# Encoder trunk on one core: the right operands of the output projection's Strassen products made during the retention instead of during the output projection

## The reference

```python
D_MODEL, SEQ, DEPTH = 1024, 1024, 2
RET_HEADS, RET_HEAD_DIM, RET_CHUNK = 4, 128, 128

for layer in range(DEPTH):
    h = rms_norm(x, norm_g[layer])
    z = h @ w_in[layer]
    qa, ka, va, ga, qr, kr, vr, gr, gm = split_columns(z)
    ...                                         # branch A: attention, SiLU gate
    ya = (jax.nn.silu(ga) * oa) @ w_branch_attn[layer]
    ...                                         # branch B: rotary on qr, kr, then
    orr = bidirectional_retention(qr, kr, vr, lg_f, lg_b)
    orr = head_group_norm(orr, ret_gn_w[layer]).astype(dt)
    yb = (jax.nn.silu(gr) * orr) @ w_branch_ret[layer]
    gates = jax.nn.sigmoid(gm).reshape(b, s, 2, d)
    merged = gates[:, :, 0] * ya + gates[:, :, 1] * yb
    x = x + merged @ w_out[layer]
return rms_norm(x, final_norm_g)
```

## Time and profile before

| | |
|---|---|
| median of 3 runs | 1848.42 us (1846.0 to 1848.89) |
| the profiled execution, its own time | 1849.25 us |
| its span | 1847.4 us, mean granted clock 0.989 |
| busy: PE, DVE, ACT, POOL | 95%, 68%, 43%, 36% of the span |
| weight loads (PEld) | 84% |
| chain that ended last | PE 73%, DVE 16%, ACT 4%, issue 4%, DMA 2%, POOL 1% |
| DMA | 113 MB, mean 61 GB/s |

### The profile page before, as it was taken

The page is one execution under the profiler, slowest core; times in us unless marked ns, Lnnn a source line. Parts: engine busy times, 40 slices in busy tenths (PEclk is TensorE's granted clock), DMA queues, the critical chain, the costliest instruction groups (busy, mean ns, idle before and its releaser), DMA issues.

```text
span 1847.4 us, 30201 instructions
## 1 busy us (share of the span) xinstructions
PE 1755.8 (95%) x10592; PEld 1556.1 (84%) x10592; DVE 1264.8 (68%) x2626; ACT 801.0 (43%) x1791; POOL 672.2 (36%) x581
## 2 busy tenths in 40 slices
PE   6999999999999999998989999999999999999986
PEld 5887878899999888887787888889999998888875
DVE  6789678725543387769986876795345544867798
ACT  4478448722123243334344873683222223433333
POOL 0157227624233323223601771484224322232240
PEclk9999999999999999999999999999999999999998
DMA  7000000011011323224130001001011023222322
GB/s 270 24 12 13 28 23 24 25 46 47 23 34 35 131 70 96 81 93 157 46 118 24 24 1 50 12 13 47 24 46 45 27 88 114 71 78 86 131 80 92
DMA packets 136665, 113.08 MB, mean 61 GB/s; under 512 B 16480, under 2 KB 115040, under 8 KB 136544
## 3 DMA queue, kind: packets, MB, share of 16 engines
q1 hardware_dynamic: 134144, 106.20, 18.0%
q10 hardware_dynamic: 2400, 5.31, 0.8%
HBM read 90.52 MB, written 20.97 MB: 60 GB/s over the span
## 4 chain that ended last, share of the span: by engine, by line
PE 73%; DVE 16%; ACT 4%; issue 4%; DMA 2%; POOL 1%; SPq 0%; DVEq 0%; ACTq 0%; POOLq 0%
PE ps L758 17%; PE ps L760 17%; PE ps L759 17%; PE ps L894 5%; PE ps L883 4%; PE ps L907 3%; PE ps L909 3%; DVE xh L2173 2%; PE ps L1000 2%; DVE pT_lo L1804 2%; PE ps L984 1%; DVE nmx L1796 1%; DVE lsum L2151 1%; DVE us L1905 1%; ACT pp L1289 1%
## 5 line engine op out<-in xcount | busy, mean ns | idle before, releaser
L758 PE MATMUL ps<-w_hi,hT_hi 128*128 128x256 f32 (+1 forms) x1280 | 391.1, 306 | 13.0 <-DVE hT_lo L1669 4.4
L760 PE MATMUL ps<-w_hi,hT_lo 128*128 128x256 f32 (+1 forms) x1280 | 376.5, 294 | 0.0
L759 PE MATMUL ps<-w_lo,hT_hi 128*128 128x256 f32 (+1 forms) x1280 | 376.3, 294 | 0.0
L758 PEld LDWEIGHTS ps<-w_hi,hT_hi 128*128 128x128 f32 x1280 | 244.9, 191 | 17.9 <-DVE hT_lo L1669 6.1
L759 PEld LDWEIGHTS ps<-w_lo,hT_hi 128*128 128x128 f32 x1280 | 245.3, 192 | 0.3
L760 PEld LDWEIGHTS ps<-w_hi,hT_lo 128*128 128x128 f32 x1280 | 244.6, 191 | 0.0
L612 POOL TENSOR_SCALAR pp<-pp,rrc 128x1024 f32<-128x1024 f32 x128 | 144.0, 1125 | 161.0 <-DVE rrc L1809 155.1
L1804 DVE TENSOR_TENSOR pT_lo<-ps,pT_hi 128x512 fp32r<-128x512 f32 x256 | 164.2, 682 | 24.4 <-ACT pT_hi L1300 22.9
L558 POOL TENSOR_SCALAR w_hi<-raw 128x1024 fp32r<-128x1024 f32 x65 | 69.1, 1063 | 286.2 <-PE ps L760 250.0
L894 PE MATMUL ps<-idf,pp 128*128 128x128 f32 x1024 | 141.5, 278 | 18.4 <-DVE pT_lo L1804 12.3
L1796 DVE TENSOR_REDUCE nmx<-ps 128x1 f32<-128x1024 f32 x128 | 154.4, 1206 | 2.6 <-PE ps L883 2.6
(11 more groups left out here) (215 smaller groups left out, 4106.8 us busy)
## 6 DMA issues: line engine op xcount, KB each, us to landing
raw<-w_in SPq DMA_DIRECT2D x167, 256.0 KB, 3.2
xs<-xh SPq DMA_DIRECT2D x2, 4096.0 KB, 16.2
ys<-y_st SPq DMA_DIRECT2D x32, 256.0 KB, 2.1
hb<-ys SPq DMA_DIRECT2D x16, 512.0 KB, 4.4
xh<-xs SPq DMA_DIRECT2D x8, 1024.0 KB, 7.4
raw<-w_a SPq DMA_DIRECT2D x16, 256.0 KB, 3.2
raw<-w_r SPq DMA_DIRECT2D x16, 256.0 KB, 3.3
w<-w_o SPq DMA_DIRECT2D x4, 1024.0 KB, 6.1
```

Source lines behind the costliest of these rows:

```text
L758: nc.tensor.matmul(outp, ah, bh, start=(start and i == 0), stop=False)
L759: nc.tensor.matmul(outp, ah, bl, start=False, stop=False)
L760: last = nc.tensor.matmul(outp, al, bh, start=False, stop=(stop and i == len(pairs) - 1))
```

## The change

The right operands of a layer's seven products are now made while its retention runs, in 28 steps: four quarters of 128 rows in each quadrant (`k`, `K_R` = 4), and in each quarter the seven products in the order `R_ORDER`. A step makes 128x512 numbers of `hi` and of `lo`. It takes three engines: GpSimd's `right_sum` adds or subtracts two blocks (20 of the 28 steps; the others use a block as it is), ScalarE casts, VectorE subtracts (`right_lo`). One tile later ScalarE issues a DMA that stores `hi` and `lo` (512 KB) to a DRAM tensor `wos`. A quarter's raw weights (1 MB) come by a DMA on ScalarE's queue, `right_load(k)`: the first ahead of head 0's first pass, the others once the quarter before is used up.

The places are numbered 2·8·h + t in a first pass and + 8 in a second; there are 56 (the second pass of the last head has none). The table puts steps at k·13 + 2 + {0, 2, 3, 5, 6, 8, 9}: 2, 4, 5, 7 in the first pass of head 0, 17, 18, 20, 21, 23 in that of head 1, 33, 34, 36, 37 in head 2, 49, 50 in head 3, the other thirteen in second passes. The sum stands one place ahead, behind that tile's add and fill; the cast stands at the top of the tile on ScalarE, the subtraction at the top of the tile on VectorE.

In the output stage the whole of `right_sum`, `right_hi` and `right_lo` is gone. SyncE's `right_in(p)` loads the finished operand of a product, 2 MB in four DMAs, into a slot when it is free; TensorE waits for these DMAs (`o_r`) where it waited for `o_blo`. So 14 MB are stored and 14 MB loaded in each layer beside the 4 MB of `w_o` that were loaded before too. The retention's loops over heads on ScalarE, VectorE and GpSimd are written out instead of looped, TensorE's is unchanged.

```diff
+K_R = 4
+R_ORDER = (1, 5, 0, 2, 3, 4, 6)
+R_PLACES, R_LOAD = (0, 2, 3, 5, 6, 8, 9), 10
+R_AT = {2 + (R_LOAD + 3) * k + o: k * N_P + i for k in range(K_R) for i, o in enumerate(R_PLACES)}
+R_LOADS = {2 + (R_LOAD + 3) * k + R_LOAD: k + 1 for k in range(K_R - 1)}
...
 # GpSimd
+                def right_sum(place):
+                    if place + 1 not in R_AT:
+                        return
+                    n = R_AT[place + 1]
+                    blocks = RIGHT[R_ORDER[n % N_P]]
+                    if len(blocks) == 1:
+                        return
+                    pool.wait_ge(r_in, 16 * (L * K_R + n // N_P + 1))
+                    r_free(pool, L, n)
...
+                    nc.gpsimd.tensor_tensor(r_total(n), a, b, ALU.add if q > 0 else ALU.subtract).then_inc(r_sum, 1)
...
                                 fill_lo(i % 2, i, n0 + U_C + fills * N_C + N_C + i)
+                        right_sum(2 * T * h + t)
...
 # ScalarE
+                def right_steps(place):
+                    if place - 1 in R_AT:
+                        n = R_AT[place - 1]
+                        act.wait_ge(r_hi, L * N_R + n + 1)
+                        act.wait_ge(r_lo, L * N_R + n + 1)
+                        a, k = 2 * (n % 2), n // N_P
+                        act.dma_start(wos[R_ORDER[n % N_P], :, :, 512 * k:512 * k + 512],
+                                      quad(ur_lo, 4)[:, a:a + 2].bitcast(F32)).then_inc(r_out[n % 2], 16)
+                    if place in R_LOADS:
+                        right_load(R_LOADS[place])
+                    if place in R_AT:
...
+                        nc.scalar.copy(r_rows(n)[0], r_src(n)).then_inc(r_hi, 1)
...
                 def first_pass(h, done):
                     for t in range(T):
+                        right_steps(2 * T * h + t)
...
 # VectorE
+                def right_lo(place):
+                    if place in R_AT:
+                        n = R_AT[place]
+                        dve.wait_ge(r_hi, L * N_R + n + 1)
+                        hi, lo = r_rows(n)
+                        V.tensor_tensor(lo, r_src(n), hi.bitcast(F32), ALU.subtract).then_inc(r_lo, 1)
...
                 def first_pass(h, done):
                     for t in range(T):
+                        right_lo(2 * T * h + t)
                         if done is not None and 2 <= t <= 3:
                             cross(done, 2 * t - 4)
...
                 add_up(0)
-                right_lo(2)
                 left_lo(3)
                 add_up(1)
-                right_lo(3)
                 left_lo(4)
...
 # SyncE
+                for p in range(3, N_P):
+                    if p != 4:
+                        sp.wait_ge(o_done, L * (4 * N_P) + 4 * N_P + 4 * ({3: 0, 5: 1, 6: 2}[p] + 1))
+                    right_in(p)
```

More of the change, by code:

```diff
@@ L111, in build @@
 def build(nc, x, gains, w_in, qn, kn, decays, gn_w, w_a, w_r, w_o,
-          ident, rope_a, rope_r, dist, idx, xs, ys, out):
+          ident, rope_a, rope_r, dist, idx, xs, ys, wos, out):
     with ExitStack() as ctx:
@@ L168, in build @@
             pT_lo = sb(p2, "pT_lo", [2, T, 256], F32R)
+        with ExitStack() as pz:
+            sb(pz, "below_wo", [2 * SEQ])
+            wo_raw = sb(pz, "wo_raw", [4, 512])
         ur_hi = sb(ctx, "ur_hi", [KA, SEQ], F32R)
@@ L200, in build @@
             pp = sb(pp_, "pp", [3, SEQ])
-        with ExitStack() as pw:
-            w21 = sb(pw, "w21", [4, 512])
         hb = sb(ctx, "hb", [2, DM])
@@ L205, in build @@
             w12 = sb(pg, "w12", [4, 512])
+        with ExitStack() as pg:
+            first_r = sb(pg, "first_r", [4, 512], F32R)
         gB = sb(ctx, "gB", [DM])
@@ L249, in build @@
             "g_sum", "g_hi", "g_wd", "g_wp", "g_p", "g_a", "g_d", "g_t"))
[L250 to L253 removed]
+        o_r = [[sem("o_r%d%d" % (i, h)) for h in range(2)] for i in range(4)]
+        r_in, r_sum, r_hi, r_lo = map(sem, ("r_in", "r_sum", "r_hi", "r_lo"))
+        r_out = [sem("r_out0"), sem("r_out1")]
+        o_sum, o_ahi, o_alo, o_done, o_post = map(sem, ("o_sum", "o_ahi", "o_alo", "o_done", "o_post"))
         f_y = sem("f_y")
@@ L354, in build, with right_wide @@
         quad = lambda t_, a: t_[:].rearrange("p a (b c) -> p (a b) c", c=512)[:, a:a + 4]
-        w22 = raw[:].rearrange("p a k (b c) -> p (a k b) c", c=P).rearrange("p (a b) c -> p a (b c)", b=4)
-        w11, w11b = w1x[:, 0:4], w1x[:, 4:8]
-        right_raw = (w12[:], w11, w11b, w11b, w11, w22, w11)
+        def right_wide(p, h):
+            return 256 if p in IN_W and (p, h) != (0, 0) else 512
         def right_slot(p, h):
+            if (p, h) == (0, 0):
+                return first_r[:, 0:2], first_r[:, 2:4]
             if p in IN_W:
@@ L508, in _, with right_in @@
                 y_back(1)
-                def block(kh, c, k0=0, kn=4):
-                    src = w_o[bass.ds(L * DM, DM), c * 512:(c + 1) * 512].rearrange("(k p) c -> p k c", p=P)
-                    return src[:, 4 * kh + k0:4 * kh + k0 + kn]
+                def right_in(p, halves=(0, 1)):
+                    for h in halves:
+                        c = right_wide(p, h)
+                        for s, to in enumerate(right_slot(p, h)):
+                            src = wos[p, :, s, 1024 * h:1024 * h + 1024].rearrange("p (b c) -> p b c", c=c)
+                            sp.dma_start(to.bitcast(F32), src).then_inc(o_r[R_SLOT[p]][h], 16)
                 def x_block(r, c):
@@ L675, in _ @@
                 rotate(0, None)
-                with pool.Fori(0, RH - 1) as h:
+                for h in range(RH - 1):
                     fill_qk(h)
+                    for t in range(T):
+                        right_sum(2 * T * h + T + t)
                     rotate(h + 1, h)
@@ L1142, in last_product @@
                     pe.wait_ge(o_alo, L * (2 * N_P) + 2 * ORDER_A.index(p) + 2)
-                    pe.wait_ge(o_blo, L * (2 * N_P) + 2 * N_P + 2 * p + 2)
+                    for h in range(2):
+                        pe.wait_ge(o_r[R_SLOT[p]][h], 32 * (L * R_USES[R_SLOT[p]] + R_NTH[p] + 1))
                     for i in range(4):
@@ L1399, in second_pass @@
                             update(h, t - 1)
+                right_load(0)
                 first_pass(0, None)
-                with act.Fori(0, RH - 1) as h:
+                for h in range(RH - 1):
                     second_pass(h)
@@ L1941, in normed @@
                     V.tensor_tensor(oc[:, o], oc[:, o], g2[:, o], ALU.mult).then_inc(c_yg, 1)
+                def right_lo(place):
+                    if place in R_AT:
+                        n = R_AT[place]
+                        dve.wait_ge(r_hi, L * N_R + n + 1)
+                        hi, lo = r_rows(n)
+                        V.tensor_tensor(lo, r_src(n), hi.bitcast(F32), ALU.subtract).then_inc(r_lo, 1)
                 def keep_out(h, half):
+                    if h >= 2:
+                        for b in range(2):
+                            dve.wait_ge(r_out[b], 16 * (L + 1) * (N_R // 2))
                     dve.wait_ge(consts_in, NCONST)
@@ L1984, in _ @@
                 first_pass(0, None)
-                with dve.Fori(0, RH - 1) as h:
+                for h in range(RH - 1):
                     second_pass(h)
@@ L2189, in _ @@
                 merge_a(K - 1, 0)
-                right_lo(0)
                 give(K - 1, 4)
```

155 lines of the change are left out of this document (58 added, 97 removed).

## The result

The changed kernel takes 1894.92 us (median of 5 runs, 1894.18 to 1899.34), the kernel before 1848.89 in the same comparison: ratio 1.0252, interval 1.024 to 1.0263. It is slower by 46 us. The prediction said 1885, range 1862 to 1903, slower.

The account below looks back on a forecast made before the run. TensorE was taken to bound the retention, VectorE the output projection. From the profiled 1849.25, +57 for the retention, −24.2 for the output stages and +4 for the clock gave 1886.1, 0.8 over the median, so 1885; range 1862 to 1903.

Parts of the forecast that it names:

- What bounds what: Retention: TensorE full, 29.39 of 30 us; output projection: VectorE full, 10.00 of 10, TensorE with holes.
- Output stage: Output projections of both layers: TensorE's holes go, about 12.1 us a layer, −24.2 in all.
- What VectorE would shed: Output projection: VectorE loses fourteen subtractions and the slowdown beside GpSimd's sum, at least 18.6 of 90 us.
- Rivals 2 and 4: Output stage: 2, operands late, +3.5 a layer, 1892, chance 0.10; 4, half the gain, +12, 1897, 0.10 with Rival 3.
- Waiting in the retention: First passes: TensorE waits for the serial chain of each step, 28.5 us a layer, +57 in all.
- The hole at the third cross term: Head 1, first pass: TensorE's next cross waits for the banks of the first, 3.4 us.
- tiles 6 and 7: Head 1, first pass: rotations of tiles 4 and 5 come late for TensorE, 1.4 and 1.3, together 2.7 us.
- Second passes: Retention: the thirteen steps there cost nothing; if that cover fails, some 0.5 a step, 6 a layer.
- Clock: Granted clock falls after retention holes, 6.8 us; falls of the output stages go, about 3.4; taken as +4.
- Rival 3: Retention: the clock falls after every hole, +10 more, 1895; chance 0.10 together with rival 4 of the output stage.
- The page's exclusion: Retention: each of 20 sums could hold up a subtraction or scan step 1.3 us, 1 or 2 us more a head.
- Rival 1: Retention: TensorE's spare bank covers the chain, so it costs 0; 1824, chance 0.08.

Follow-up runs that it names:

- subtraction last: Changed kernel with VectorE's subtraction in first passes moved from the top of the tile to its end; 1845.75 us.
- transfers-alone kernel: Changed kernel without sums, casts, subtractions and the waits for them; loads and stores stay, a fixed copy is stored; 1821.69 us.
- the best order tried: Changed kernel with the subtraction at the end of the tile in first passes and the 28 steps at other places; 1835.96 us.

## Why the prediction was right, and where its sizes were off

**What bounds what.** Right. The output projection was VectorE's and its holes went; the retention was TensorE's, and its spare bank didn't cover the chain. That the same instructions in another order (subtraction last) give 1845.75 shows it for the retention, the transfers-alone kernel (1821.69) for the output projection.

**Output stage, forecast −24.2.** Measured −25.0. The two parts on which it rested are seen: no `o_r` wait in the products (no idle time over 0.05 us between 875.31 and 953.37, though most pieces of an operand, 512 KB each, landed 9.5 to 11 us after issue, with others issued around them), and VectorE 63.27 of 78.06 us, no longer full. What VectorE would shed was taken too small: 23.4 us went (86.68 less 63.27) where 18.6 of 90 were worked out; it bounded nothing any more either way. Rivals 2 and 4 fall.

**Waiting in the retention, forecast 28.5 a layer.** Measured 25.2 and 25.4 (27.5 and 27.9 less the 2.3 and 2.6 that stood there before). By head, layer 0, idle forecast and measured: 6.5 and 5.7, 8.7 and 7.9, 8.5 and 7.4, 4.8 and 4.1, each somewhat too large. In head 0 the step at place 4 was given a sum that it doesn't have (it uses a block as it is), and the first cast began at 377.1, which with this trace's 2.4 us of lead is 379.5 and not 379.9. The hole at the third cross term was forecast 3.4 and is 2.94; tiles 6 and 7 2.7 and 2.5; the second pass of head 1 1.9 and 1.6. Second passes had no holes but those at their start, as forecast.

**Clock, forecast +4.** This is the term that failed. The windows give 10.6 and 8.2 us (0.04 of 264.7 and 0.03 of 274.4), 18.8 in all; the account above leaves 21.7 beside the idle time (72.3 less 50.6), and the 2.9 between the two were not taken apart. Two errors: two of five holes were taken to be followed by a fall, and of the eight places where TensorE had stood still for 2.7 us or more it was seven (only head 3's in layer 0 stayed at 1.00); and 3.4 were taken off for the falls in the output stages, which were already in the 24.2. Against the forecast: waiting −6.4, clock with what was not taken apart +17.7, output −0.8, start −2.4, sum +8.1, from 36.8 to 44.9. So it was in part luck that the time lies only 10 us over the forecast: the waiting, taken too large, and the start hid about 9 us of the clock. Rival 3 was nearer than the 0.10 that it shared with rival 4: with its price the forecast would have been 1895.

**The page's exclusion.** I weighed the rule that a VectorE instruction with two SBUF inputs and a GpSimd instruction that reads SBUF shut each other out for the whole instruction (the Trainium skill, SBUF — State Buffer, Who interferes with whom) and let it move only the upper end. For the subtractions of the change as it is that was right, because the serial chain itself kept the two apart: 40 subtractions behind a sum took 0.734 us on average. For the scan it was not. In heads 2 and 3 a sum stands at tile 0, beside the scan (VectorE, GpSimd, TensorE; the same six instructions took 3.30 us in the earlier trace rows):

```profile
499.58 4.21 DVE L1935 SCALAR_TENSOR_TENSOR us<-us,dcur 128x128 f32<-128x128 f32 x6
```

```profile
501.56 1.31 POOL L700 TENSOR_TENSOR w1x<-wo_raw 128x512 f32<-128x512 f32 x1
```

```profile
503.85 0.48 PE L1022 MATMUL ps<-us,qkT 128*128 128x256 f32 x1 [1.51 <-DVE us L1935]
```

TensorE waits 1.51 us for it where it waits 0.61 in head 1, so the exclusion had 0.9 us in each of these heads, 3.6 of the 50.6 in all; "1 or 2 us more a head" was too much, nothing too little. Once the chain was broken the same rule showed in the experiments: 2.21 us beside `fill_lo`, and in the kernel with the subtraction last the stretched norm (1.61 and 1.62 us of idle in layer 0) and the scan, about 5 of the 9 us of idle. The rows agree with the page: the VectorE instruction is done only when the GpSimd one has ended. They show it for `L1961` as well, which has one SBUF input (0.83 in place of 0.20).

**Rival 1** (the spare bank covers it, 1824) fell. Its time is that of a retention at no cost, and the transfers-alone kernel (1821.69) shows that the output stage's gain would indeed be kept then; with the chain in place the best order tried is at 1835.96.

What is not settled: of the 14 us between 1835.96 and 1821.69 the traces name about 5 a layer of waits; the rest was not taken apart. Steps in second passes alone, and two steps in a tile, were not tried.

## What to carry to other kernels

Work moved into the idle time of an engine isn't free by that alone; it depends on where it stands in that engine's order. Put it behind the tile's own critical instructions, never at the top, if it waits for another engine. Here the change cost 46 us with the first passes' subtractions at the top of a tile, and gave 3 us with them at its end. Follow the whole chain of a step (here four engines deep) against the number of banks that decouple the bounding engine, and price each hole in the full engine at its length plus what the clock takes behind it, here 25 us of idle and 8 to 11 of clock a layer. And look at which instructions two engines run side by side: moving one out of a queue can put it beside another that shuts it out.
